# Normalised rows written in the weights' word order: stepped reads in the norm, unstepped blocks for the transposes

## The reference

```python
def rms_norm(x, g, eps=RMS_EPS):
    xf = x.astype(jnp.float32)
    y = xf * lax.rsqrt(jnp.mean(xf * xf, axis=-1, keepdims=True) + eps)
    return (y * g.astype(jnp.float32)).astype(x.dtype)

x = x + even_mixer(rms_norm(x, ev_norm[j]), ev_w_in[j], ...)        # layer 0
x = x + mla_mixer(rms_norm(x, od_norm[j]), positions, mla_w_in[j], ...)   # layer 1
x = x + hierarchical_moe(rms_norm(x, ffn_norm[layer]), moe_w_group[layer], ...)
# experts: (silu(xb @ w1[e]) * (xb @ w3[e])) @ w2[e], xb the rows routed to e
```

## Time and profile before

| | |
|---|---|
| median of 3 runs | 1603.41 us (1601.07 to 1606.24) |
| the profiled execution | 1601.44 us, span 1599.4 us |
| TensorE matmuls busy | 1359.2 us, 85% of the span |
| VectorE busy | 479.5 us, 30% |
| ScalarE, GpSimd busy | 294.5 us, 317.6 us |
| mean granted TensorE clock | 0.944 |
| HBM read | 454.59 MB |

### The profile page before, as it was taken

One profiled execution on the slowest core, in us unless ns is written; L12 is line 12 of the kernel. 1 busy time (PEld: TensorE's weight loads), 2 busy tenths in 40 slices (PEclk: granted clock), 3 DMA queues, 4 the chain that ended last, 5 costly groups with the idle time before them and its releaser, 6 DMA issues.

```text
span 1599.4 us, 19482 instructions
## 1 busy us (share of the span) xinstructions
PE 1359.2 (85%) x6164; PEld 629.8 (39%) x6164; DVE 479.5 (30%) x960; ACT 294.5 (18%) x580; POOL 317.6 (20%) x427
## 2 busy tenths in 40 slices
PE   5989999988878788788699899989987777878786
PEld 4556454333323233333364555453332322323232
DVE  6997125111111111111615573261111111111114
ACT  3245111110100101011235552111110010100100
POOL 6313001332222221221000000012322222222220
PEclk8999999999999989999899899999999998999999
DMA  6413815999999999999500305087999999999996
GB/s 216 194 70 123 338 71 190 396 382 405 406 405 404 398 408 402 414 392 359 212 12 42 119 1 210 0 323 306 397 397 404 401 392 405 404 408 398 393 379 236
DMA packets 83523, 472.37 MB, mean 295 GB/s; under 512 B 13970, under 2 KB 16194, under 8 KB 32912
## 3 DMA queue, kind: packets, MB, share of 16 engines
q1 hardware_dynamic: 69792, 445.25, 70.3%
q0 software_dynamic: 11952, 20.14, 3.8%
q10 hardware_dynamic: 1728, 6.29, 1.0%
HBM read 454.59 MB, written 27.39 MB: 301 GB/s over the span
## 4 chain that ended last, share of the span: by engine, by line
PE 44%; SPq 32%; DVE 10%; issue 6%; DMA 6%; ACT 2%; DVEq 0%; POOL 0%; POOLq 0%; ACTq 0%
SPq L1644 21%; PE ps L1439 14%; SPq L1649 11%; PE ps L1459 6%; DMA ring<-in_moe_w 4%; PE ps L441 3%; PE ps L875 2%; PE ps L895 2%; PE ps L315 2%; PE ps L899 2%; PE ps L430 2%; PE ps L390 2%; PE ps L1429 1%; DVE smalls L541 1%; DVE extra L541 1%
## 5 line engine op out<-in xcount | busy, mean ns | idle before, releaser
L1439 PE MATMUL ps<-ring,region_b 128*64 128x512 f32 x1408 | 347.8, 651 | 82.5 <-issue 53.3
L1439 PEld LDWEIGHTS ps<-ring,region_b 128*64 128x64 f32 x1408 | 118.0, 149 | 309.3 <-issue 269.1
L1576 DVE TENSOR_TENSOR extra<-extra,ps 128x256 f32<-128x256 f32 x64 | 27.0, 422 | 603.5 <-ACT extra L1514 573.8
L1439 PE MATMUL ps<-wbuf,region_b 128*64 128x512 f32 x320 | 160.7, 661 | 39.0 <-DMA region_a<-in_moe_w 21.5
L1459 PE MATMUL ps<-ring,extra 128*64 128x512 f32 x704 | 160.8, 598 | 34.5 <-DVE extra L1582 32.9
L1439 PE MATMUL ps<-region_a,region_b 128*64 128x512 f32 x320 | 160.9, 662 | 0.0
L1383 POOL DMA_INDIRECT region_b<-hrow,icol x120 | 111.5, 930 | 147.8 <-issue 147.8
L1395 POOL DMA_INDIRECT ytok<-extra,icol x120 | 105.9, 882 | 153.8 <-issue 153.8
L1514 ACT ACTIVATE extra<-ps 128x256 f32<-128x256 f32 x64 | 24.6, 385 | 587.0 <-PE ps L1439 551.5
L1589 DVE COPY extra<-ps 128x512 f32<-128x512 f32 x64 | 44.3, 692 | 241.1 <-PE ps L1459 241.1
L1439 PEld LDWEIGHTS ps<-wbuf,region_b 128*64 128x64 f32 x320 | 47.0, 151 | 146.8 <-issue 137.5
(11 more groups left out here) (309 smaller groups left out, 1563.1 us busy)
## 6 DMA issues: line engine op xcount, KB each, us to landing
ring<-in_moe_w SPq DMA_DIRECT2D x264, 1024.0 KB
wbuf<-in_moe_w SPq DMA_DIRECT2D x80, 1024.0 KB
region_a<-in_moe_w SPq DMA_DIRECT2D x40, 1024.0 KB
ytok<-ring SPq DMA_DIRECT2D x8, 1024.0 KB, 10.2
wbuf<-in_ev_w_in SPq DMA_DIRECT2D x3, 2048.0 KB, 17.5
wbuf<-in_ev_w_out SPq DMA_DIRECT2D x2, 2048.0 KB, 14.4
hrow<-region_a ACTq DMA_DIRECT2D x8, 512.0 KB, 10.9
region_a<-ytok SPq DMA_DIRECT2D x8, 512.0 KB, 6.0
```

What stands on the lines that cost most here:

```text
L1439: last = TE.matmul(ps[CAP * g:CAP * (g + 1), 2 + j, :], xtr[j][:, k, CAP * g:CAP * (g + 1)], up_weights(2 * slot + g, k), start=k == 0, st ...
```

## The change

The norm's product writes h with its columns already sorted by k, so that block k of h is contiguous: x and gain are read with a step of 8 words, h is written without one. The transposes of h, and those of the gathered rows, which carry the same order through hrow, then take blocks without a step. The overflow path (L1710) uses the same function for its blocks. The evictions, the DMAs, the weights and everything behind the transposes are unchanged.

```diff
+        def by_weight(v):
+            return v.rearrange("p (q k) -> p k q", k=KC)
+
         def norm_rows(n, c):
 ...
-            V.scalar_tensor_tensor(h[:, c, :], x[:, c, :], rstd[:, c:c + 1], gain[:, :],
-                                   ALU.mult, ALU.mult).then_inc(s_h, 1)
+            V.scalar_tensor_tensor(h[:, c, :].rearrange("p (k q) -> p k q", k=KC), by_weight(x[:, c, :]), rstd[:, c:c + 1],
+                                   by_weight(gain[:, :]), ALU.mult, ALU.mult).then_inc(s_h, 1)
 ...
         def norm_transposes(n, c):
             TE.wait_ge(s_h, TC * n + c + 1)
-            hs = h[:, c, :].rearrange("p (q k) -> p k q", k=KC)
+            hs = h[:, c, :].rearrange("p (k q) -> p k q", k=KC)
 ...
         def xin_block(j, k):
-            return xin[j].rearrange("p (q k) -> p k q", k=KC)[:, k, :]
+            return xin[j][:, k * P:(k + 1) * P]
```

## The result

The changed kernel takes 1611.13 us (median of 8 runs) where the kernel before takes 1604.05 in the runs beside it: ratio 1.0043, 95% interval 1.0031 to 1.0056, so 5.0 to 9.0 us slower, 6.9 in the middle. The interval lies just beyond the 0.3% bound. The profiled execution of the changed kernel took 1613.12 us (span 1611.3), the slowest of its eight; that of before, 1601.44, was among the fastest. The two profiles are therefore 11.9 us apart, and some of that isn't the change's.

A forecast was written before the change was run, and what follows sets the result against it. First expert pairs bound by TensorE, the long middle by the weight stream. Norm costs 4.6 + 0.8 + 6.0 + 0.8 = 12.2 us, less 0.3 for transposes, on 1603.4 gave 1615 us, range 1604 to 1620.

The forecast's parts named there:

- What bounds the kernel: Expert stage: first pairs bound by TensorE, long middle by the weight stream; a delay ahead of it is not taken back.
- The sum: Costs of the four norms added: 10d - 2.8, 12.2 us with d = 1.5, less 0.3 for the transposes.
- The transposes: Gathered rows and norm: unstepped weight loads gain 0.05 us a burst at most, 0.3 us for the kernel.
- The product's price: Norm's product on VectorE: two reads stepped by 8 words make each instruction 2.8 us in place of 1.285.
- d: Extra time of each norm product from the stepped reads: 1.5 us taken, 0.76 as the lower end.
- one price: Rival: the two stepped reads run side by side, so d = 0.76 and the kernel takes 1608 us; chance 0.26.
- What of d reaches the end: Norm by norm, the part of d not covered by waits: 4.6 + 0.8 + 6.0 + 0.8 = 12.2 us.
- 4d: Norm 2: VectorE is the path and nothing covers any of the four products; 6.0 us.
- 4d - 1.38: Norm 0: d for the fourth product, 3d for the first three less a 1.38 us wait; 4.6 us.
- d - 0.7: Norms 1 and 3: only the fourth product counts, with 0.7 us of cover; 0.8 us each.
- The clock: Rival: longer waiting in norm 2 leaves TensorE at half clock, another 3.8 us, 1619 us; chance 0.08.
- hidden after all: Rival: part of norm 0 or 2 is taken back; without norm 0's 4.6 us, +7.4, 1611 us; chance 0.08.

The follow-up runs named there:

- x only: Changed kernel with norm weights laid out in word order by the host, so one stepped read in place of two: 1610.77 us, ratio 1.0036.
- The fill: Unread 256-column matmuls on TensorE during norm 2's waits: added to the changed kernel 1607.22 us, ratio 1.0022; added to the kernel before 1602.07 us, 0.9987.
- The filler without a step: Kernel before with one more unstepped VectorE product of 560 elements ahead of each of the 16 norm products: 1608.93 us, ratio 1.0031.
- the filled change: Changed kernel with 17 unread TensorE matmuls in norm 2 (10, 4 and 3 ahead of blocks 1, 2 and 3): 1607.22 us, ratio 1.0022.

## Why the prediction was right, and where it was off

**What bounds the kernel: right.** The expert stage kept its pace and its rate, and it took back nothing of what was lost ahead of it. From the first up-projection to norm 2's first reciprocal the changed kernel even takes a little longer, 788.59 - 272.19 = 516.4 us against 783.35 - 268.09 = 515.3. The six profiles with a delayed norm 0 have 515.5 to 516.7 us there, the five others 515.0 to 515.5. The sum has no term for this 1 us or so, and no run shows what makes it.

**The transposes: right, with a bound a little low.** A burst of 8 after a wait takes 1.16 us before; in the changed kernel the first one of pair 1 takes 1.09:

```profile
279.21 1.09 PE L1432 MATMUL ps<-con,region_b 128*128 128x128 f32 x8
```

That is 0.07 us, where the prediction had 0.05 as the most. It matters little, since these bursts lie under the weight stream: with all 512 of them unstepped and norms 0 and 2 as before, the ratio is 1.0001 (0.9989 to 1.0012). The 0.3 us that the prediction took off for them is too small for these runs to show.

**The product's price: the step that failed.** "I take the upper end, d = 1.5 us an instruction": it is 0.79. That is the rival called one price, to which the prediction gave 0.26. Both reasons for it fell. Each read does not pay by itself (x only: 2069 ns), and going on for 128 steps costs no more than the router's sum with its 8: the product pays 0.79 / 1024 = 0.77 ns an element, the row of L1279 gave 0.74. The nearest row was right as it stood, and I argued it away. The Trainium skill (Vector Engine (DVE) Microarchitecture Reference, 5.2 Measured stream behaviour on trn2) gave 1.75 and 2.50 ns a column for two kinds of steps. The traces agree with both: the measured (2055 - 213) / 1024 = 1.80 for 8 words is near the first and (2772 - 213) / 1024 = 2.50 for 24 words is the second, to the digit, 213 ns being what a product without a step takes beyond 1024 x 1.047. The figure for 24 words, the one that fitted my d of 1.5, holds for 24 words and not for 8. The rule that the prediction took from that section of the Trainium skill, a full rate only in runs of two adjacent words, doesn't hold here: single words with a step of 2 take 1285 ns, as without a step.

**What of d reaches the end: right, with small corrections.** Norm 2 is 4d (3.1 us). Norm 0 is 1.5 us where 4d - 1.38 makes 1.8: the third product of before had itself started 0.2 us late (12.48 - 10.86 is 1.62, and the spacing of the first two is 1.39), which was cover that the row with the wait didn't show, and the first product of before started 0.06 us later than that of the changed kernel. Norms 1 and 3 lose about 0.2 us each, where d - 0.7 makes 0.1, and the wait of 0.8 us that the prediction expected there with d = 1.5 isn't seen. GpSimd's work did move along with VectorE's, as argued.

**The clock: a rival that came true in part.** At the right d the sum gives 10 x 0.79 - 2.8 - 0.3 = 4.8 us. Most of the rest is the clock's in the projection: 2.6 us in the mean of the delayed profiles against 0.5 in the others. With the measured terms it is 1.5 + 3.1 + 0.4 + 2.1 = 7.1 us, against 6.9 (5.0 to 9.0). The fill gives the clock only 1.3 us, and the 1 us or so of the expert stage isn't in this sum, so the good fit is no proof of the 2.1. The prediction gave this 8 in 100 and tied it to d = 1.5; it needs only 3 us of delay. Its ground against it, that the clock comes back with the first full burst, held in the profile it was read from (1.00) and not in that of the changed kernel, where the first 8 us without a gap got 0.67. The filler without a step shows it (0.68 of the clock), and so does the filled change (1.00). The range would have held with the right d and no clock at all, 1604.05 + 4.8 = 1609: it was wide enough for the lower price. What is luck is how near the forecast came. Two errors went against each other, a product priced twice too dear and a clock priced at nothing in the likeliest case, and without the second the loss would stand at the edge of the 0.3% bound. The 1611 of the rival "hidden after all" is met by chance too: no part of norm 0 or norm 2 was taken back by what runs behind it.

**Still open:** how often a kernel with the short norm 2 loses clock in the projection (one of three profiles did), and so whether the clock's share in the 6.9 us is nearer to 1.3 or to 2.1; what makes the first expert stage about 1 us longer behind a delayed norm 0; and why 24 words cost twice what 8 and 16 do.

## What to carry to other kernels

When a stepped access is unavoidable, ask first which engine is waited for in that stage: here it was moved from TensorE's weight loads, where it was covered to 0.07 us in a burst, to VectorE products of which eight lay bare. Price it by the nearest row with the same step, even if that row has one stepped operand and the change has two. And when a delay of some microseconds is put ahead of a dense TensorE stage, look at the granted clock on both sides of it: here 1.3 to 2.1 us of this change's 6.9 were there, and a few unread matmuls in the gaps took them back, together with 0.8 us in the transposes that the kernel before loses as well.

## What the runs showed of the hardware

- VectorE reads single words with a step of 2 at full rate (1285 ns for 1024 elements), and pairs every 8 words too. Two operands with the same step cost what one costs.
- The price of larger steps isn't monotone: 2024, 2055, 1933, 2772 and 2176 ns for 4, 8, 16, 24 and 32 words.
- A weight load for a transpose takes 140 ns when its columns lie in a row, 193 with a step of 8, and its matmuls follow each other every 0.11 us either way.
- After norm 2's waits, TensorE ran a stretch without a gap (8.00 us of 8.00 busy) that was granted 0.64 to 0.73 of its clock when VectorE had kept it waiting 3 us longer, and 1.00 in two of three profiles when it hadn't; with unread matmuls in the waits it was granted 1.00 in each of three.
